# Finishing the second residual norm inside each expert pass of a hybrid RWKV-7 and mixture-of-experts layer

## What is computed

```python
scores = sigmoid(x1 @ router_w)
# the best of 4 groups of 8 experts, and in it the best 2 experts of the token
gate = scores[expert] / sum(scores[expert])
for the 2 experts e of each token t:
    h = silu(x1[t] @ w_gate[e]) * (x1[t] @ w_up[e])        # 1024 -> 512
    y[t] += gate * (h @ w_down[e])                         # 512 -> 1024
out = layer_norm(ALPHA * x1 + y, ln2_g, ln2_b)             # over the 1024 of a token
```

## Time and profile before

| | |
|---|---|
| median of 3 runs | 1126.53 us (1126.05 to 1126.75) |
| the profiled execution's own time | 1125.88 us |
| its span in the profile | 1124.2 us |
| PE busy | 982.6 us, 87% of the span |
| DVE, ACT, POOL busy | 359.7, 166.8, 123.9 us |
| transfers | 261.35 MB, mean 232 GB/s |

### The profile page before, as it was taken

How to read it: one execution, slowest core, us unless ns; L and a number is a source line. 1 busy time by engine, 2 the same in 40 slices (tenths; PEclk the granted TensorE clock), 3 DMA queues, 4 the chain that set the end, 5 groups by cost and what they waited for, 6 DMA issues and landing times.

```text
span 1124.2 us, 15343 instructions
## 1 busy us (share of the span) xinstructions
PE 982.6 (87%) x5932; PEld 457.0 (41%) x5933; DVE 359.7 (32%) x674; ACT 166.8 (15%) x304; POOL 123.9 (11%) x192
## 2 busy tenths in 40 slices
PE   7999999999999999999993688888888888887840
PEld 3644475466456457444453233333333333322210
DVE  0695643553463373422445000110000000000018
ACT  1123322312222222200001000000010000000010
POOL 1000010010010010033000111111111111111100
PEclk9999999999999999999995799999999999999985
DMA  8232201211220210573537799999999999999982
GB/s 254 61 92 58 74 22 38 76 39 39 56 58 21 66 48 10 213 295 151 219 115 322 270 420 419 396 419 421 419 419 418 419 421 419 420 420 421 420 316 117
DMA packets 90430, 261.35 MB, mean 232 GB/s; under 512 B 11192, under 2 KB 56248, under 8 KB 65552
## 3 DMA queue, kind: packets, MB, share of 16 engines
q1 hardware_dynamic: 83936, 249.46, 57.4%
q0 software_dynamic: 5648, 9.07, 2.2%
q10 hardware_dynamic: 800, 2.15, 0.5%
HBM read 256.97 MB, written 12.85 MB: 240 GB/s over the span
## 4 chain that ended last, share of the span: by engine, by line
PE 63%; SPq 14%; DVE 10%; DMA 8%; issue 4%; ACT 2%; DVEq 0%; ACTq 0%; POOLq 0%; PEldq 0%
SPq L450 13%; PE proj L1219 11%; PE bank L1464 10%; PE proj L1178 10%; PE bank L1484 6%; PE proj L1399 5%; PE bank L1309 5%; PE bank L1387 5%; DMA xT_sb<-w_gu 3%; DMA arena<-w_gu 2%; DMA gates<-y_rows 2%; PE proj L1186 1%; PE proj L1197 1%; DVE arena L867 1%; DVE arena L1117 1%
## 5 line engine op out<-in xcount | busy, mean ns | idle before, releaser
L1219 PE MATMUL proj<-xT_sb,ring 128*128 128x512 f32 x384 | 182.1, 607 | 0.0
L1110 DVE TENSOR_TENSOR const<-pass_sb,bank 128x256 f32<-128x256 f32 x33 | 13.9, 422 | 408.4 <-ACT pass_sb L718 408.4
L1464 PE MATMUL bank<-arena 128*64 128x512 f32 x544 | 122.2, 596 | 16.2 <-PE bank L1484 11.3
L1178 PE MATMUL proj<-xT_sb,ring 128*128 128x512 f32 (+1 forms) x272 | 119.1, 594 | 0.0
L1219 PEld LDWEIGHTS proj<-xT_sb,ring 128*128 128x128 f32 x384 | 68.2, 189 | 68.3 <-issue 64.8
L1464 PEld LDWEIGHTS bank<-arena 128*64 128x64 f32 x544 | 43.0, 137 | 95.2 <-issue 82.7
L1178 PEld LDWEIGHTS proj<-xT_sb,ring 128*128 128x128 f32 (+1 forms) x272 | 50.8, 188 | 64.6 <-issue 64.5
L1464 PE MATMUL bank<-gates,arena 128*64 128x512 f32 x256 | 59.7, 617 | 8.2 <-PE bank L1484 4.7
L1309 PEld LDWEIGHTS bank<-arena 64*64 64x64 f32 x1536 | 52.8, 134 | 18.2 <-ACT arena L676 9.1
L1309 PE MATMUL bank<-arena 64*64 64x64 f32 (+1 forms) x1536 | 56.5, 228 | 0.0
L1387 PE MATMUL bank<-branches,arena 128*128 128x512 f32 x128 | 55.4, 593 | 0.9 <-DVE branches L961 0.9
(11 more groups left out here) (259 smaller groups left out, 1011.1 us busy)
## 6 DMA issues: line engine op xcount, KB each, us to landing
arena<-w_gu SPq DMA_DIRECT2D x64, 1024.0 KB, 24.6
gates<-w_gu SPq DMA_DIRECT2D x32, 1024.0 KB, 21.9
arena<-w_down SPq DMA_DIRECT2D x24, 1024.0 KB, 24.7
ring<-w_in SPq DMA_DIRECT2D x42, 512.0 KB, 3.9
gates<-w_down SPq DMA_DIRECT2D x16, 1024.0 KB, 23.5
branches<-w_down SPq DMA_DIRECT2D x16, 1024.0 KB, 25.9
xT_sb<-w_gu SPq DMA_DIRECT2D x16, 1024.0 KB, 26.4
ring<-w_gu SPq DMA_DIRECT2D x16, 1024.0 KB, 25.8
```

Of the source, the lines that this page charges most:

```text
L1178: ins = pe.matmul(proj[0:w, b, :], ring[:, slot, k, 0:w], xT_sb[:, k, :], start=(k == 0), stop=(k == KT - 1))
L1219: ins = pe.matmul(proj[:, gate_at["bank"], :], ring[:, gate_at["slot"], k, :], xT_sb[:, k, :], start=(k == 0), stop=(k == KT - 1))
L1464: ins = pe.matmul(bank[SLOTS * h:SLOTS * h + SLOTS, 0, :], xeT[:, k % 4, SLOTS * (k // 4):SLOTS * (k // 4) + SLOTS], gu[k // 2][:, k % 2, ...
```

## The change

A token's upper expert always comes in a later pass than its lower one, and the change uses that. DRAM now holds only the lower experts' rows (`y_dram` has half the rows, and POOL fills it with zeros early in the program, 8 transfers of 256 KB). A pass writes the rows of tokens for which it is the lower expert to `y_dram`, and the finished rows of tokens for which it is the upper one to the output. Everything after the last pass is gone: the loads of x1, ln2, lower and upper rows, the norm over four blocks of tokens and the four stores.

In a pass p:

- ACT computes `x_half`, ALPHA / 2 times the gathered tokens (`half_rows`), for the next pass; it waits for the `y_e` of this pass, since that reads the single `x_half`. It also takes the root of the variance, and loads its table for Sqrt and back for Silu.
- DVE takes over the product with the gate and adds `x_half` to it (`finish`), so that both experts' rows together hold ALPHA times x1. Then it adds the lower rows gathered into `y_low`, and does the norm in slot order on 128 x 512: statistics of each half row, PE adds up those of the two halves (`pair_stats`), DVE finishes the norm with the gains kept in PSUM.
- POOL: `scatter_lower(p)`, then the gather of pass p + 2, then `scatter_out(p)`, then the gather of the lower rows for pass p + 1. `next_tokens` has one more wait, for `s_base`, that is for `x_half`. The gather of a pass's tokens is issued from `one_pass(p)` as `next_tokens(p + 1)`, behind `scatter_lower(p)`.

```diff
             def next_tokens(p):
                 pool.wait_ge(s_xe, p * 16 + 16)
                 pool.wait_ge(s_xeTp, p + 1)
+                pool.wait_ge(s_base, p + 1)
                 gather(p + 1)
...
-            def one_pass(p):
-                next_tokens(p + 2)
-                pool.wait_ge(s_yst, p * 16 + 16)
-                scatter(p + 1)
+            def lower_rows(p, first=False):
+                pool.tensor_copy(up_now[:, 0:1], up_tab[:, bass.ds(p, 1)]).then_inc(s_up, 1)
+                pool.wait_ge(s_up, p + 1)
+                if not first:
+                    pool.wait_ge(s_yst, p * 16)
+                pool.sem_inc(s_begun, 1)
+                pool.indirect_dma_start(y_low, None, y_dram, bass.IndirectOffsetOnAxis(ap=up_now[:, 0:1], axis=0),
...
+            def scatter_lower(p):
+                pool.tensor_copy(low_now[:, 0:1], low_tab[:, bass.ds(p, 1)]).then_inc(s_low, 1)
+                pool.wait_ge(s_low, p + 1)
                 pool.wait_ge(s_ye, p + 2)
...
+            def scatter_out(p, first=False):
+                if not first:
+                    pool.wait_ge(s_ost, p * 16)
+                pool.tensor_copy(out_now[:, 0:1], up_tab[:, bass.ds(p, 1)]).then_inc(s_outidx, 1)
+                pool.wait_ge(s_outidx, p + 1)
+                pool.wait_ge(s_x2, p + 1)
...
+            def one_pass(p, first=False):
+                scatter_lower(p)
+                next_tokens(p + 1)
+                scatter_out(p, first)
+                pool.wait_ge(s_ylow, p * 16 + 16)
+                lower_rows(p + 1)
...
+            def half_rows(p):
+                act.wait_ge(s_xe, p * 16 + 16)
+                act.wait_ge(s_ye, p + 1)
+                act.activation(x_half, xe, ACT.Copy, scale=ALPHA / 2).then_inc(s_base, 1)
 
             def one_pass(p):
                 act.activation(warm[:, 1:2], warm[:, 0:1], ACT.Silu)
                 act.wait_ge(s_hp, p + 1)
-                act.activation(h_silu, bank[:, 0, 0:FE // 2], ACT.Silu).then_inc(s_silu, 1)
-                act.wait_ge(s_yp, p + 2)
+                act.activation(h_e, bank[:, 0, 0:FE // 2], ACT.Silu).then_inc(s_silu, 1)
+                half_rows(p + 1)
+                act.activation(warm[:, 2:3], warm[:, 0:1], ACT.Sqrt)
+                act.wait_ge(s_dev, p + 1)
+                act.activation(half_rs[:, 2:3], pair[:, 1:2], ACT.Sqrt, bias=half_rs[:, 1:2], scale=0.5).then_inc(s_root, 1)
...
+            def finish(p, first=False):
+                dve.wait_ge(s_yp, p + 2)
+                dve.wait_ge(s_base, p + 1)
+                if not first:
+                    dve.wait_ge(s_yst, p * 16)
+                dve.scalar_tensor_tensor(y_e, bank[:, 1, :], gate_tab[:, bass.ds(p, 1)], x_half, MUL, ADD).then_inc(s_ye, 1)
+                dve.wait_ge(s_ye, p + 2)
+                dve.wait_ge(s_ylow, p * 16 + 16)
+                if not first:
+                    dve.wait_ge(s_ost, p * 16)
+                dve.tensor_tensor(x2, y_e, y_low, ADD).then_inc(s_norm2, 1)
+                dve.wait_ge(s_norm2, p * 5 + 1)
+                dve.bn_stats(ln_stat[:, 0, 0:6], x2).then_inc(s_norm2, 1)
+                dve.wait_ge(s_norm2, p * 5 + 2)
+                dve.memset(half_rs[:, 3:4], 0.0)
+                dve.bn_aggr(half_mv, ln_stat[:, 0, 0:6]).then_inc(s_stat, 1)
+                dve.wait_ge(s_pair, p + 2)
+                dve.tensor_scalar(mean, pair[:, 0:1], 0.5, None, MUL)
+                dve.scalar_tensor_tensor(dev_in, pair[:, 0:1], -0.5, half_mv[:, 0:1], MUL, ADD).then_inc(s_norm2, 1)
+                dve.wait_ge(s_norm2, p * 5 + 3)
+                dve.tensor_scalar(dev_in, dev_in, dev_in, LN_EPS, MUL, ADD).then_inc(s_dev, 1)
+                dve.scalar_tensor_tensor(x2, x2, mean, ln2_g, SUB, MUL).then_inc(s_norm2, 1)
+                dve.wait_ge(s_root, p + 1)
+                dve.reciprocal(root, root).then_inc(s_norm2, 1)
+                dve.wait_ge(s_norm2, p * 5 + 5)
+                dve.scalar_tensor_tensor(x2, x2, root, ln2_b, MUL, ADD).then_inc(s_x2, 1)
...
+            with dve.Fori(1, N_EXP) as i:
+                products(i)
+                finish(i)
...
+            def pair_stats(p):
+                pe.wait_ge(s_stat, p + 1)
+                for h in range(2):
+                    ins = pe.matmul(pair[SLOTS * h:SLOTS * h + SLOTS, :], C("ident_twice"), ln_mv[:, 0, :], start=True, stop=True)
+                ins.then_inc(s_pair, 1)
...
                 for k in range(KT):
+                    if k == 4:
+                        pair_stats(p)
```

More of the change, by code:

```diff
@@ L284, in program @@
         xeT = cut(T, r="p (c s) -> p c s", k=dict(c=4))
[L285 to L299, removed]
+        xe, h_e = pass_sb[:, 0:T], pass_sb[:, T:T + FE // 2]
+        hT = h_e.rearrange("p (c s) -> p c s", c=2)
+        ln2_g, ln2_b = proj[:, 0, :], proj[:, 1, :]
+        pair = bank[:, 3, FE // 2:FE // 2 + 2]
+        at = CONSTS["ident_twice"][0] + CONSTS["ident_twice"][1]
+        y_e, y_low = const[:, at:at + T], const[:, at + T:at + 2 * T]
+        assert at == P + P // 2 and at + 2 * T <= TABLE.shape[1]
         place = {"late": 0, "raw": 0}
@@ L315, in program @@
         assert place["late"] <= 2 * RW + 2 * T
+        gate_tab = late("raw", raw_flat, PASSES)
+        idx_tab, up_tab, low_tab, idx_now, up_now, low_now, out_now, more_i, extra_i, first_i = (
+            late("raw", raw_flat, n).bitcast(I32) for n in (PASSES, PASSES, PASSES, 1, 1, 1, 1, 1, N_EXP, N_EXP))
+        warm = late("raw", raw_flat, 3)
+        at = place["raw"]
+        x2, x_half = raw_flat[:, at:at + T], raw_flat[:, at + T:at + 2 * T]
+        assert at + 2 * T <= RAW
         chosen = late("raw", raw_flat, (TT + 1) * N_EXP).rearrange("p (c e) -> p c e", c=TT + 1)
@@ L442, in _ @@
                 load(2, c, 2)
+            sp.wait_ge(s_more, 1)
+            for i, dst in ((0, y_e), (1, x2)):
+                for h in range(2):
+                    at = 2 * SGU + 2 * D + D * i + T * h
+                    sp.dma_start(dst[SLOTS * h:SLOTS * h + SLOTS, :],
+                                 rows[:, at:at + T].partition_broadcast(SLOTS).rearrange("p a d -> p (a d)")).then_inc(s_lnback, 16)
             def reload(e, b, used):
@@ L486, in _ @@
                                pattern=[[0, 4], [1, P]], channel_multiplier=-1).then_inc(s_masked, 1)
+            for n in range(T // SLOTS):
+                pool.dma_start(y_dram.rearrange("(n s h) d -> n s (h d)", s=SLOTS, h=2)[n], zeros).then_inc(s_y0, 16)
             pool.wait_ge(s_early, 1)
@@ L553, in _ @@
+            def one_pass(p, first=False):
[4 more added lines that the diff above has]
+                lower_rows(p + 1)
             gather(0)
+            pool.wait_ge(s_more, 1)
+            pool.memset(y_low, 0.0).then_inc(s_xe0, 1)
             next_tokens(0)
-            next_tokens(1)
-            scatter(0)
-            with pool.Fori(0, N_EXP - 2) as i:
+            pool.wait_ge(s_xe0, 2)
@@ L558, in _ @@
+            pool.wait_ge(s_y0, 16 * (T // SLOTS))
+            lower_rows(0, first=True)
+            one_pass(0, first=True)
+            with pool.Fori(1, N_EXP - 1) as i:
                 one_pass(i)
-            pool.wait_ge(s_more, 1)
             more = pool.value_load(more_i[0:1, 0:1], min_val=0, max_val=MORE)
@@ L562, in _ @@
                 with pool.Fori(0, more) as i:
-                    one_pass(i + (N_EXP - 2))
+                    one_pass(i + (N_EXP - 1))
+            scatter_out(more + (N_EXP - 1))
+            pool.wait_ge(s_ost, more * 16 + 16 * N_EXP)
             pool.wait_ge(s_yst, more * 16 + 16 * (N_EXP - 1))
-            scatter(more + (N_EXP - 1))
+            pool.wait_ge(s_ylow, more * 16 + 16 * N_EXP)
             pool.wait_ge(s_xe, more * 16 + 16 * (N_EXP + 1))
@@ L736, in _ @@
                 with act.Fori(0, more) as i:
[L737 to L740, removed]
+                    one_pass(i + N_EXP)
         @block.vector
@@ L1119, in _ @@
             turned(0)
-            with dve.Fori(0, N_EXP) as i:
-                one_pass(i)
-            dve.wait_ge(s_more, 1)
+            dve.sem_inc(s_ye, 1)
+            dve.sem_inc(s_stat, 1)
+            products(0)
+            dve.wait_ge(s_lnback, 64)
+            dve.tensor_copy(ln2_g, y_e)
+            then(dve.tensor_copy(ln2_b, x2))
+            finish(0, first=True)
+            with dve.Fori(1, N_EXP) as i:
+                products(i)
+                finish(i)
             more = dve.value_load(more_i[0:1, 0:1], min_val=0, max_val=MORE)
```

122 lines of the change are left out of this document (44 added, 78 removed).

## The result

| | median | ratio to the kernel before |
|---|---|---|
| before | 1126.29 us (1125.04 to 1126.75) | |
| the change | 1231.12 us (1226.45 to 1233.91) | 1.0933 (1.0914 to 1.0951) |
| forecast | 1171 us (1135 to 1220) | |

A forecast was written before the change was run, and what follows sets the result against it. PE and transfers, both close to full, were taken to bound the passes, then the last norm. 32 passes of 16.1 us lose 74 us, the end gains 28.6: +45, to 1171 us, range 1135 to 1220.

The forecast's parts named there:

- The ring: Passes: chain from one `y_e` to the next through POOL's scatter and token gather, 16.1 us a pass where PE needs 13.4.
- `y_e` to scatter: First term in each pass: end of `y_e` to the start of POOL's lower scatter, 0.80 us.
- to the gather's start: In each pass, `y_e` to the token gather's start: 0.80 us, plus 1.02 scatter issue, plus 0.97 after the index copy.
- `x2` done: Norm in each pass: `x2` done about 6 us after `y_e`, before `h` is wanted at 7.5 us.
- The end: After the last `y_e`: 11.0 us in place of 39.6, a gain of 28.6 us.
- The zero fill: Early in the program, POOL's 2 MB of stores near 22 us: cost 0, or at most 5 us.
- the ln2 rows: Start of the passes: 0.5 MB load and two DVE copies, costed at nothing; if late, one slip of a few us.
- `x_half`'s wait: In each pass, `x_half` ready about 0.75 us after `y_e`, inside the scatter's issue, costing nothing.
- turn to the end of `y_e`: 6.61 us: Last term in each pass: PE's turn of the tokens to `y_e` done, taken from the kernel before.
- The landing: Token gather's time to land in each pass: 6.7 us under load, the uncertain term; 6.0 to 7.3 us gives 15.4 to 16.7.
- The landing shrinks: Rival: the gather lands in 2.9 us, weights bind as before, 1097 us; chance 0.11.
- Transfers of POOL queue behind each other: Rival: the gather moves only after the scatter lands, losing 4.6 us a pass: 1318 us, half gives 1245; chance 0.12.

The follow-up runs named there:

- staged_first: Changed kernel with `x_half` staged early in a free PSUM bank and POOL's gather of tokens issued ahead of the lower scatter: 1108.29 us, 0.9844 of the kernel before.
- staged: Changed kernel with only `x_half` staged in a free PSUM bank, the gather of tokens staying behind the lower scatter: 1226.39 us in a single run.
- before_ring: Kernel before with only POOL's order swapped, the gather of tokens behind the scatter that waits for `y_e`; norm not moved: 1229.66 us, ratio 1.0929.
- gather_first: Changed kernel with only POOL's order changed, the gather of tokens ahead of the lower scatter; `x_half` still waits for `y_e`: 1166.39 us, ratio 1.0363.
- fill6: Changed kernel plus six matmuls nobody reads, ahead of each turn where PE waits for the gather: 1184.79 us, ratio 1.0531.
- light: Changed kernel with each reload of weights moving 128 of 2048 columns, all waits and POOL transfers kept: 1086.69 us in a single run.
- fill3: Changed kernel plus three matmuls nobody reads, ahead of each turn: 1201.63 us in a single run.

## Why the prediction was wrong

**What held.** The ring, with its terms: `y_e` to scatter 0.82 us (0.80 said), to the gather's start 2.84 (2.79), PE released by the landing in 27 of 32 passes. `x2` done at 5.4 us after `y_e` (6), PE not waiting for it. The end: 10.0 us (11.0). The zero fill and the ln2 rows cost at most the 2 us by which the first `y_e` is later (644.96 against 642.92). PE did not wait for weights. That the ring is what decides is shown by staged_first, and that the order on POOL closes it by staged and before_ring. The forecast was right that `x_half`'s wait costs nothing while that order stands; gather_first shows what it costs once the order is changed back.

**The step that failed.** The term "turn to the end of `y_e`: 6.61 us" was taken from a kernel whose PE hardly waits, and put into one whose PE waits 3 us in each pass. In the changed kernel it is 8.3 us in the mean: over 32 passes it adds 55 us to 211.5. I never asked what the new wait does to PE's granted clock, though a stretch with clock 0.80 stood in the trace of the kernel before at the start of the passes, where PE had waited 8.6 us for the first gather:

```profile
616.00:650.00 34.00, 22.36 (x91) 7.91 (x92) 2.35 (x7) 2.65 (x5) 5.00 (x8) 0.80 0.72 274
```

fill6 is the proof: with the clock held the turns are nearly as forecast. It still takes 14 us more than the 1171 us said; some 9 of them are the added matmuls of the last four passes, where no wait hides them.

**A term that was mis-sized.** The landing: 6.7 us said, 7.2 us measured in the mean of the 28 passes under load, then 2.2 to 3.7 us in the last four, where PE and not the ring binds. From the gather's start to the turn this is 16 us more over the 28 passes and 11 us less over the four; the way from `y_e` to the gather's start adds 2 us. 55 + 16 + 2 - 11 is the 62 us by which 577.2 is above 32 x 16.1 = 515.2.

**The rivals.** "The landing shrinks" was wrong here and right without the weights (light). "Transfers of POOL queue behind each other" was wrong as a mechanism: without the scatter the landing loses 0.4 us, not 4.6, and with four transfers a pass but no weights it is 3 us. The range did not hold 1231 us because all my bounds were on the landing, and none on PE's speed.

The Trainium skill warns of it: "TensorE: Matmul & The Clock Gate", section "HAM oscillation — how this bites in real kernels", describes a kernel that waits for a transfer between its groups of matmuls and falls back to the slow clock each time. The trace of the change agrees for 26 of its 32 passes, not for each: in the pass shown the clock is 0.50 at the start of the down product, and the turn's four transposes take 0.94 us for 0.66 at full clock. The page stood in no sentence of the forecast, and should have been a rival with a price.

## What to carry to other kernels

Before an instruction is moved behind a wait on a shared issue queue, look at what is issued after it and for whom: here a gather that had 5 us of cover went behind a wait for a result that needs the gather two steps on, and the ring of latency cost more than the whole removed tail. When a change opens a wait of microseconds on PE in every step, price it twice: the wait, and the matmuls after it at half clock (here 2.6 us in the pass shown). The repair was to copy the input out of the way at once into a free PSUM bank and to issue the gather first; then the fused norm gained 1.6% over the kernel before.

## What the runs showed of the hardware

- PE's granted clock fell to 0.50 in matmuls behind a wait, in runs with mean waits of 1.5 to 3.3 us ahead of the turn, and not in every pass: with 3.3 us turn to `y_e` was 7.7 us or more in 26 of 32 passes, with 1.5 us (gather_first) in 14, with 1.6 us (fill3) in 11. In fill6, with waits of up to 1.2 us ahead of the turn, and in the last six passes of staged_first, with waits for weights of 0.3 to 1.2 us each, it stayed at 1.00; that a wait of such a length is safe is not shown, as three slow passes of fill3 follow waits of 1.13 to 1.48 us.
- Useless matmuls in a wait saved 46 us (1231.12 to 1184.79).
- An indirect gather of 256 KB at most takes 3 us from issue to landing when little else is in flight (light), and about 7 us beside the stream of weights; with the queue of weights deep (a piece of 1 MB lands in 25 us) it was 6.7 us. With a short queue (a piece lands in some 8 us) it was 7.3 us in the change but 6.5 us in before_ring, so the depth of that queue is not what sets it; the change's surplus over before_ring comes with what the norm adds to a pass.
